# A decoder block on TensorE: the two halves of the rounded activations moved 64 and 128 bytes off a multiple of 256

## The reference, cut to what matters

```python
shift, scale, gate = jnp.split(c @ w_mod + b_mod, 3, axis=-1)
u = x * (1.0 + scale[:, None, :]) + shift[:, None, :]
proj = u @ w_in                                  # 2048 -> 12288 columns
q, k, v, z_a, cb, cc, cx, z_b, g_a, g_b = jnp.split(proj, SEG_SPLITS, axis=-1)
...                                              # differential attention (8 heads) -> o
y_a = o * silu(z_a)
y_b = cb * causal_dwconv(cc * cx, conv_w) * silu(z_b)
h = sigmoid(g_a) * (y_a @ w_proj_a) + sigmoid(g_b) * (y_b @ w_proj_b)
out = h @ w_out
y = layernorm(ALPHA * x + gate[:, None, :] * out) * ln_gain + ln_bias
```

## The kernel before

| tile | bytes | start before | over 256 | start after | over 256 |
|---|---|---|---|---|---|
| cst | 1032 | 16512 | 128 | 16512 | 128 |
| c_col | 64 | 17568 | 160 | 68096 | 0 |
| b_col | 128 | 17632 | 224 | 133760 | 128 |
| mean_mat | 512 | 17888 | 224 | 17696 | 32 |
| neg_max, row_sum | 32 each | 18656, 18688 | 224, 0 | 100928, 100960 | 64, 96 |
| stats | 384 | 18720 | 32 | 18464 | 32 |
| raw | 16384 | 19200 | 0 | 18944 | 0 |
| w_hi | 16384 | 35584 | 0 | 35328 | 0 |
| w_lo | 16384 | 51968 | 0 | 51712 | 0 |
| act_hi | 32768 | 68352 | 0 | 68160 | 64 |
| act_lo | 32768 | 101120 | 0 | 100992 | 128 |
| gate | 8192 | 133888 | 0 | 133888 | 0 |
| y_hi | 16384 | 195328 | 0 | 195328 | 0 |
| y_lo | 16384 | 211712 | 0 | 211712 | 0 |

## Time and profile before

### The profile page before, as it was taken

One profiled execution on the slowest core, in us unless ns is written; L12 is line 12 of the kernel. 1 busy time (PEld: TensorE's weight loads), 2 busy tenths in 40 slices (PEclk: granted clock), 3 DMA queues, 4 the chain that ended last, 5 costly groups with the idle time before them and its releaser, 6 DMA issues.

```text
span 1563.5 us, 18079 instructions
## 1 busy us (share of the span) xinstructions
PE 1498.8 (96%) x6600; PEld 1220.2 (78%) x6600; DVE 819.4 (52%) x1072; ACT 501.1 (32%) x693; POOL 44.0 (3%) x52
## 2 busy tenths in 40 slices
PE   2889999999999999999999999999999999999994
PEld 2667788787887878878787888888788888888883
DVE  6997764647546375463754742222522323434448
ACT  1215434425344243443434422223122221422121
POOL 0000000000000000000000000000000000000004
PEclk9999999999999999999999999999999999999997
DMA  9995432533324334233433232322232232362312
GB/s 346 382 382 155 135 108 69 147 107 107 108 85 130 107 111 123 82 114 107 132 110 94 82 135 80 107 93 96 82 107 98 90 107 80 108 254 96 107 54 108
DMA packets 215248, 200.22 MB, mean 128 GB/s; under 512 B 7729, under 2 KB 176433, under 8 KB 214449
## 3 DMA queue, kind: packets, MB, share of 16 engines
q1 hardware_dynamic: 209648, 176.52, 34.9%
q0 software_dynamic: 4608, 16.78, 3.9%
q10 hardware_dynamic: 962, 6.53, 1.0%
HBM read 195.61 MB, written 4.19 MB: 128 GB/s over the span
## 4 chain that ended last, share of the span: by engine, by line
PE 88%; DVE 7%; issue 2%; ACT 1%; DMA 1%; SPq 0%; POOLq 0%; POOL 0%; ACTq 0%; DVEq 0%
PE acc L992 28%; PE acc L993 28%; PE acc L994 28%; DVE mod_sum L631 2%; PE sc L1081 2%; DVE w_lo L604 1%; PE misc L1099 1%; DMA w_mod_in<-in_w_mod 1%; PE sc L1090 1%; DVE res L975 1%; DVE res L951 0%; ACT act_hi L431 0%; DVE gate L653 0%; PE misc L1041 0%; DVE act_lo L658 0%
## 5 line engine op out<-in xcount | busy, mean ns | idle before, releaser
L604 DVE TENSOR_TENSOR w_lo<-raw,w_hi 128x1024 fp32r<-128x1024 f32 (+1 forms) x258 | 310.6, 1215 | 599.6 <-ACT w_hi L388 599.5
L992 PE MATMUL acc<-act_hi,w_hi 128*128 128x512 f32 x1472 | 579.2, 394 | 21.8 <-DVE w_lo L604 13.9
L994 PE MATMUL acc<-act_hi,w_lo 128*128 128x512 f32 x1472 | 574.8, 390 | 0.0
L993 PE MATMUL acc<-act_lo,w_hi 128*128 128x512 f32 x1472 | 574.3, 390 | 0.0
L388 ACT ACTIVATE w_hi<-raw 128x1024 fp32r<-128x1024 f32 (+1 forms) x258 | 268.9, 1052 | 720.0 <-PE acc L994 637.9
L992 PEld LDWEIGHTS acc<-act_hi,w_hi 128*128 128x128 f32 x1472 | 277.2, 188 | 93.6 <-issue 35.8
L994 PEld LDWEIGHTS acc<-act_hi,w_lo 128*128 128x128 f32 x1472 | 277.3, 188 | 58.6
L993 PEld LDWEIGHTS acc<-act_lo,w_hi 128*128 128x128 f32 x1472 | 277.5, 189 | 56.7 <-issue 0.2
L994 PE MATMUL acc<-y_hi,w_lo 128*128 128x512 f32 x256 | 99.6, 389 | 0.0
L992 PE MATMUL acc<-y_hi,w_hi 128*128 128x512 f32 x256 | 99.6, 389 | 0.0
L993 PE MATMUL acc<-y_lo,w_hi 128*128 128x512 f32 x256 | 99.6, 389 | 0.0
(11 more groups left out here) (151 smaller groups left out, 990.9 us busy)
## 6 DMA issues: line engine op xcount, KB each, us to landing
raw<-in_w_in SPq DMA_DIRECT2D x256, 256.0 KB
w_mod_in<-in_w_mod SPq DMA_DIRECT2D x64, 512.0 KB, 6.9
raw<-in_w_tail SPq DMA_DIRECT2D x32, 1024.0 KB
raw<-in_w_in SPq DMA_DIRECT2D x29, 1024.0 KB
gate_in<-in_w_mod POOLq DMA_DIRECT2D x32, 512.0 KB, 4.2
x_in<-in_xT SPq DMA_DIRECT2D x8, 512.0 KB, 8.0
x_tok<-in_x ACTq DMA_DIRECT2D x1, 4096.0 KB, 13.2
raw<-in_w_in SPq DMA_DIRECT2D x8, 384.0 KB
```

The source lines that it names most:

```text
L604: ins = dve.tensor_tensor(w_lo[:, f % SLOTS, :, 0:width], raw[:, (f // 2) % 2, 2 * (f % 2):2 * (f % 2) + 2, 0:width], w_hi[:, f % SLOTS, : ...
L992: pe.matmul(dst, a_hi, b_hi, start=first, stop=False)
L993: pe.matmul(dst, a_hi, b_lo, start=False, stop=False)
L994: return pe.matmul(dst, a_lo, b_hi, start=False, stop=last)
```

## The change

Four small tiles change their place in the order of declarations, and nothing else: `c_col` (64 bytes) now stands in front of `act_hi`, `neg_max` and `row_sum` (64 bytes together) in front of `act_lo`, and `b_col` (128 bytes) in front of `gate`. `raw`, `w_hi` and `w_lo` move down by 256 bytes, `act_hi` by 192 and `act_lo` by 128. The table above has the places. No instruction is added, removed or reordered.

```diff
         cst = sb("cst", [P, C_WIDTH])
-        c_col = sb("c_col", [P, KT])
-        b_col = sb("b_col", [P, 2 * KT])
         conv_col = sb("conv_col", [P, HEADS * 3])
...
         row_max = sb("row_max", [P, 4])
-        neg_max = sb("neg_max", [P, 8])
-        row_sum = sb("row_sum", [P, 8])
         stats = sb("stats", [P, NT, D // COLS, 6])
...
         w_hi = sb("w_hi", [P, SLOTS, 2, COLS], F32R)
         w_lo = sb("w_lo", [P, SLOTS, 2, COLS], F32R)
+        c_col = sb("c_col", [P, KT])
         act_hi = sb("act_hi", [P, KT, T], F32R)
+        neg_max = sb("neg_max", [P, 8])
+        row_sum = sb("row_sum", [P, 8])
         act_lo = sb("act_lo", [P, KT, T], F32R)
+        b_col = sb("b_col", [P, 2 * KT])
         gate = sb("gate", [P, D])
```

## The result

The changed kernel takes 1589.42 us (1587.79 to 1590.04, 4 runs), the one before 1564.65 us beside it (1563.51 to 1565.96, 4 runs): a ratio of 1.0156, with a 95% interval of 1.0139 to 1.0174. It is 24.8 us slower, and the two profiled spans differ by the same 24.8 us (1588.3 and 1563.5).

The account below looks back on a forecast made before the run. The prediction took PE's matmul stream, 226.7 ns from start to start, to bound the kernel. Its terms summed 0 + 0 + 0 + 0 = 0 on the median, giving 1564.4 us, with a range of 1530 to 1592.

Parts of the forecast that it names:

- likeliest case: PE's matmul distance stays 226.7 ns, so no change: 1564.4 us, own range 1561.5 to 1567.5, chance 0.40.
- rival 1: Matmuls with act tiles: unequal offsets lengthen steps to 232 ns, +26 us, 1590.6 us; chance 0.33.
- its row's price: Steps around mean_mat, mean of ten 232 ns, +5.3 each; over 4916 matmuls with act tiles, +26 us.
- What bounds the kernel: PE's stream from 165 to 1532 us: time is the number of matmuls times a start-to-start distance of 226.7 ns.
- The value that I take is 0: The 4916 matmuls with act tiles: their distance stays unchanged, 0 us, between bounds of -65.5 and +26 us.
- If only the low part does it, a third, +9 us: Matmuls with act tiles: if only the low half's offset lengthens steps, the loss is a third, +9 us.
- Rival 2: Matmuls with act tiles: offsets part colliding reads, removing all excess, -65.5 us, or half, -33 us, 1531.6; chance 0.27.
- The three other zeros: Small tiles, DVE and ACT work on act tiles, and mean_mat's move: 0 each, mean_mat at most 0.4 us.
- The rule of 16-byte lines: PE's tile reads: memory is read in 16-byte lines, so moving by 64 or 128 bytes sums to 0.
- The two independent read ports: PE's moving-operand and load reads use separate ports, which spoke against any collision and for 0.

Follow-up runs that it names:

- sizes: TensorE's matmul stream by itself with fewer columns loaded or moving; at 512 moving, 226.7 ns a matmul rises to 231.7 with 32 columns loaded.
- The stream alone: Separate kernel where only TensorE works, blocks of 128x512 fp32r matmuls at chosen tile offsets; 226.7 ns a matmul at 0/0, 232.3 at 64, 128, 64 over 0.
- both64: Against the kernel before: act_hi and act_lo both 64 bytes past a multiple of 256, weights and y on it; 1577.70 us, ratio 1.0091.
- both128: Against the kernel before: act_hi and act_lo both 128 bytes past a multiple of 256, the rest on it; 1593.33 us, ratio 1.0187.
- w64: Against the kernel before: w_hi and w_lo 64 bytes past a multiple of 256, act and y tiles on it; 1598.03 us, ratio 1.0220.
- lo128: Against the kernel before: only act_lo offset, 128 bytes past a multiple of 256; 1586.27 us, ratio 1.0145.
- keep256: Against the kernel before: the four small tiles moved in front of gate; raw, weights and act move by 256 bytes, staying on multiples; 1564.17 us, ratio 1.0003.
- all64: Against the kernel before: raw, weights and act tiles all 64 bytes past a multiple of 256, y on it; 1570.96 us, ratio 1.0046.
- hi64: Against the kernel before: only act_hi offset, 64 bytes past a multiple of 256; 1595.22 us, ratio 1.0201.
- offsets: TensorE's matmul stream by itself, 33 blocks of 48 matmuls, each with its own moving and stationary offsets; 226.7 ns at 0/0, 228.8 at 64 over 0.
- pairs: TensorE's matmul stream by itself, 24 blocks of 96 matmuls, moving and stationary offsets alternating in either order; both orders slow; 0, 128, 0 over 0 takes 228.9 ns.

## Why the prediction was right or wrong

**The likeliest case failed, its range held, and rival 1 is what happened.** I had put 0.40 on no change and 0.33 on rival 1, at 1590.6 us (my own sum, 1564.4 + 26, gives 1590.4); measured is 1589.4. The range of 1530 to 1592 held only because it had been stretched to take in rival 1 at its row's price. The time that I gave was 25 us too low, and the no-change case's own range, 1561.5 to 1567.5, was missed by 22 us.

**What bounds the kernel** was right: a longer distance between starts went into the time one for one (24.6 of 24.8 us), with PE busy throughout.

**The step that failed** is "The value that I take is 0", for the matmuls with act tiles. The runs show +5.1 ns with act moving and +4.4 with act stationary in its place, 24.4 us in all. It rested on three readings. The first: 544 cycles for 2048 + 512 bytes look like a rate of reading, to which the load adds a fixed 32 cycles. The sizes run speaks against that: at 512 moving columns the distance rises, from 226.7 to 231.7 ns, when the load shrinks to 32 columns. The second: the distance is the same for all tiles, slots and columns. That was true and empty, since every place in these loops is a multiple of 256 and the steps between them are multiples of 512, as the text itself said. The third: in the earlier trace rows the steps stay long after the stationary tiles are back in place, so the address need not be the cause. The stream alone shows that they can be the trace of an address. After a block with another offset, a block at 0/0 takes 235, 225, 230, 236, 229, 232 and 231 ns before it settles at 226.7. The ten steps of the earlier trace rows, read in ns from the trace (six starts are left out of the rows, not four), are 235, 233, 234 and then the same 235, 225, 230, 236, 229, 232 and 231. The disturbance outlasts its cause by some seven matmuls; that was a property of the effect, and I had counted it against it. No run has `mean_mat` on a multiple of 256, so the cause of the steps of the earlier trace rows itself is argued from this likeness.

**The price of rival 1** was right by its row: +5.3 ns a step, taken from the ten around mean_mat, against 5.1 measured with act moving and 4.4 with act stationary; +26 us against +24.8. It was a fair sample by luck as well as by sense, since other offsets give 2 to 10 ns more than 226.7, and one gives nothing. Its mechanism was half right. Equal offsets of the two halves (both64, both128) cost too, as does an offset of the weights (w64).

**"If only the low part does it, a third, +9 us"** was wrong: lo128 took +22.4. The stream has more than one pattern for the same places. In lo128 the act part of one merge group, 192 matmuls from 896.19 us, has 231.1 ns, and the next, from 962.33 us, has 228.9, with the same instructions on tiles of the same remainders:

```profile
896.19 0.40 PE L992 MATMUL acc<-act_hi,w_hi 128*128 128x512 f32 x1
...
940.56 0.40 PE L992 MATMUL acc<-y_hi,w_hi 128*128 128x512 f32 x1
...
962.33 0.39 PE L992 MATMUL acc<-act_hi,w_hi 128*128 128x512 f32 x1
...
1006.28 0.39 PE L992 MATMUL acc<-y_hi,w_hi 128*128 128x512 f32 x1
```

The second of these is what a price per matmul gives: a third of the 6.7 ns by which 128 over 0 is slower. The first is twice that. A price per matmul of one kind, added up, is therefore no safe way to size a mixture.

**Rival 2 (faster) has nothing for it.** In none of the blocks and kernels is a settled distance at 512 columns under 226.7 ns; what the 13.3 ns above 213.3 are stays open. The 215.8 ns that the Trainium skill (TensorE: Matmul & The Clock Gate, section Back-to-back issue gap) gives to 512 columns when a matmul stands alone were reached nowhere here.

**The three other zeros** were right: keep256 is at 1.0003, and L658, L907 and L431 kept their durations. For `mean_mat` the traces say it directly: the steps around it are 53 ns longer than 226.7 each in sum before, and 54 in keep256, where it stands 32 past a multiple.

**The rule of 16-byte lines** (the Trainium skill, SBUF — State Buffer, section Door 1: The DMA port swizzle) would have expected 0 for this change, since 64 bytes change no count of lines. The measurement decides against it as a guide to places. The two independent read ports that the Trainium skill gives PE (SBUF — State Buffer, section Who interferes with whom) don't let one expect it either: all64 slowed the products with y from 226.7 to 233.3 ns by moving the weights under them. What the two reads share is not shown by any run here.

**What stays open** is the mechanism. Shown is where it sits (in TensorE's own reads, with no other engine at work), what it depends on (the offsets among all tiles of the stream, repeating after 256 bytes), and that it keeps a state over several matmuls. Why 16 over 16 is slow and 0 over 16 isn't, no run explains. All blocks write to the same four tiles of PSUM in turn; other outputs were not tried.

## What to carry to other kernels

Where a kernel is a dense stream of fp32r matmuls of 128x128 by 128x512, give every tile that TensorE reads, weights and activations alike, the same remainder over 256 bytes (0, 32, 64 and 128 were tried in the stream alone and are equally good); here that is worth 0.5 to 2.2% against seven other placements, and it costs a look at the sizes of the small tiles declared in front. A small tile declared between the big ones shifts only those behind it, and can cost that much without any change in the instructions. When a control in the trace varies only in steps that leave the suspected quantity untouched, it is no evidence, however many cases it has.

## What the runs showed of the hardware that had not been expected

- Settled distances form short repeating patterns whose mean is a fixed number: 226.67 ns for agreeing tiles, and 228.89, 231.11, 232.22 and 233.33 ns in the kernels with others (lo128 twice, changed, hi64). Where a pattern could be made out, which is in nearly all blocks, its sum is a multiple of 6.67 ns, 16 cycles of 2.4 GHz: 3 x 228.89 = 103 x 6.67, 3 x 231.11 = 104 x 6.67.
- The same instructions on the same places can settle in either of two patterns (lo128: 231.1 and 228.9 ns; the stream 0, 128, 0 over 0: 233.4 ns in `offsets` and 228.9 in `pairs`; 128 over 0: 233.5 in `offsets` and 232.4 in `sizes`). So a single distance for a placement, as in the table of blocks, is one of the values that it can take.
- After a block with another offset, a stream whose tiles agree finds back to 226.7 ns within one to ten matmuls, at a cost of up to some 40 ns in all. Each of the blocks at 0/0, 32/32, 64/64 and 128/128 ended there, whatever stood before it.
- The gain from agreement was seen at 512 moving and 128 loaded columns and doesn't carry over to the other sizes as a rule: with 128 columns loaded, moving offsets of 0, 64 and 128 over 0 give 173.3, 173.3 and 176.0 ns at 384 and 120.0, 117.8 and 118.7 ns at 256, where 0 is the slowest. At the lower clock level (1.2 GHz, granted clock 0.50) the distance is 427 ns and there is no excess to begin with the earlier trace rows.
